# Two thirds of a block's closing gate-and-adds move from VectorE to ScalarE and Pool

## The reference

```python
x = x + g_f * peer_ffn(modulate(rmsnorm(x, norm_ffn_w[i]), sh_f, sc_f), ...)

def block(xc):                                   # 128 tokens at a time
    ...                                          # scores, two top-16s: 8 heads x 16 experts of 16384 for each token
    g = jax.nn.softmax(best_s, axis=-1).astype(xc.dtype)
    act = jax.nn.gelu(jnp.einsum("cd,chkd->chk", xc, u_tab[e]))
    return jnp.einsum("chk,chkd->cd", g * act, v_tab[e])
```

## Time and profile before

| | us |
|---|---|
| median of 3 runs (lowest to highest) | 2940.29 (2937.99 to 2942.69) |
| the profiled execution's own time | 2935.12 |
| its span | 2933.3 |
| TensorE busy | 2632.2 (90%) |
| VectorE busy | 1990.6 (68%) |
| Pool busy | 1349.4 (46%) |
| ScalarE busy | 1043.5 (36%) |

### The profile page before, as it was taken

How to read it: one execution, slowest core, us unless ns; L and a number is a source line. 1 busy time by engine, 2 the same in 40 slices (tenths; PEclk the granted TensorE clock), 3 DMA queues, 4 the chain that set the end, 5 groups by cost and what they waited for, 6 DMA issues and landing times. The chain is left out here.

```text
span 2933.3 us, 36691 instructions
## 1 busy us (share of the span) xinstructions
PE 2632.2 (90%) x12550; PEld 2159.5 (74%) x12550; DVE 1990.6 (68%) x4287; ACT 1043.5 (36%) x2939; POOL 1349.4 (46%) x1076
## 2 busy tenths in 40 slices
PE   4789889999999999999965888999999999999992
PEld 2544558888888888888854766888888887878881
DVE  2356249998877866666674247998877775666667
ACT  3335142269878700000004423229888830000000
POOL 0000034455666666666550005365666674655562
PEclk7889999999999999999987989999999999999996
DMA  7247133799999999999991223599999999999995
GB/s 304 65 189 303 43 116 130 289 384 380 356 410 409 409 404 409 409 409 409 409 375 57 86 71 117 207 374 366 360 384 409 407 407 404 409 409 409 409 409 212
DMA packets 246591, 917.87 MB, mean 313 GB/s; under 512 B 27120, under 2 KB 32272, under 8 KB 239120
## 3 DMA queue, kind: packets, MB, share of 16 engines
q0 software_dynamic: 147456, 536.94, 46.6%
q1 hardware_dynamic: 94800, 374.54, 33.1%
q10 hardware_dynamic: 4160, 4.19, 0.4%
HBM read 909.27 MB, written 6.29 MB: 312 GB/s over the span
## 5 line engine op out<-in xcount | busy, mean ns | idle before, releaser
L1199 PE MATMUL exp_down<-peer_gates,all_ring 128*128 128x256 f32 x2720 | 613.3, 382 | 22.3 <-DMA all_ring<-in_peer_v 22.3
L1172 PE MATMUL exp_out<-peer_both,all_ring 128*128 128x256 f32 x2752 | 617.4, 380 | 9.4 <-DMA all_ring<-in_uT 5.7
L1199 PEld LDWEIGHTS exp_down<-peer_gates,all_ring 128*128 128x128 f32 x2720 | 508.0, 190 | 117.1 <-DMA all_ring<-in_peer_v 50.5
L1172 PEld LDWEIGHTS exp_out<-peer_both,all_ring 128*128 128x128 f32 x2752 | 515.9, 190 | 83.1 <-DMA all_ring<-in_uT 11.8
L1090 POOL DMA_INDIRECT all_xT<-in_u_rows,peer_eidx x278 | 350.4, 1260 | 169.6 <-DVE peer_dots L1548 115.6
L1555 DVE SCALAR_TENSOR_TENSOR peer_both<-all_xT,peer_dots,peer_both 128x1024 f32<-128x1024 f32 x226 | 290.3, 1285 | 147.7 <-DMA all_xT<-in_peer_v,peer_eidx 144.1
L1548 DVE CUSTOM_DVE_ANT_0 all_xT<-all_xT,peer_both 128x1024 f32<-128x1024 f32 x278 | 338.1, 1222 | 66.9 <-DMA all_xT<-in_u_rows,peer_eidx 65.2
L1063 POOL TENSOR_TENSOR ask_w_lo<-all_ring,ask_w_hi 128x1024 fp32r<-128x1024 f32 x22 | 52.5, 2390 | 675.4 <-ACT ask_w_hi L1227 675.4
L1090 POOL DMA_INDIRECT all_xT<-in_peer_v,peer_eidx x230 | 271.3, 1180 | 176.8 <-DVE peer_both L1555 144.3
L1199 PE MATMUL exp_down<-peer_gates,spare_ring 128*128 128x256 f32 x1376 | 315.6, 382 | 13.9 <-DMA spare_ring<-in_peer_v 13.9
L1299 ACT ACTIVATE spare_heavy<-all_iota_b,spare_index 128x128 f32<-128x128 bf16 x1024 | 314.2, 411 | 0.0
(11 more groups left out here) (288 smaller groups left out, 3843.0 us busy)
## 6 DMA issues: line engine op xcount, KB each, us to landing
all_ring<-in_uT SPq DMA_DIRECT2D x172, 512.0 KB, 6.8
all_ring<-in_peer_v SPq DMA_DIRECT2D x170, 512.0 KB, 6.8
mix_raw<-in_ada_tiles SPq DMA_DIRECT2D x48, 1024.0 KB, 9.6
spare_ring<-in_peer_v SPq DMA_DIRECT2D x86, 512.0 KB
spare_ring<-in_uT SPq DMA_DIRECT2D x84, 512.0 KB
all_ring<-in_w_peer_q SPq DMA_DIRECT2D x22, 512.0 KB, 3.7
all_ring<-in_w_gs_in SPq DMA_DIRECT2D x16, 512.0 KB, 3.7
all_ring<-in_w_in SPq DMA_DIRECT2D x12, 512.0 KB, 3.7
```

The source lines that it names most:

```text
L1172: mm = nc.tensor.matmul(outs[:, c % 2, 0:DENSE], raw[c % R][:, k, :], hd[:, k, :], start=(k == 0), stop=(k == KD - 1))
L1199: mm = nc.tensor.matmul(dn[:, m, :], raw[at % R][:, m, :], gates[:, :, c, :], start=(c == 0 and m % 2 == 0), stop=(c == NKEYS - 1), skip_g ...
```

## The change

ScalarE multiplies by the gate: it reads `dn` (eight 128x256) once the last dense product is done, and block 0's transposed sum (eight 128x128), and writes both to SBUF, into columns 0 to 23 of `gates`, which nobody reads any more by then. Pool adds the old stream and writes `xT`: a dense add behind each of the last eight fetches (slots 504 to 511), then eight adds for block 0. The first dense add also waits for the stream to be back and for slots up to 495 to be used. So that `xT` can be written this early, its four row buffers take no slot from 496 on (`TAIL` = 16). VectorE keeps block 1's eight gate-and-adds; it no longer waits for `s_used` and `s_mm` before them, only for the transposes. Nothing else is changed, and the arithmetic is the same but for the rounding between multiply and add.

```diff
--- before.py
+++ after.py
@@ -944,6 +944,7 @@
         PAIRS = NKEYS // 2
         NEAR = 262
         FIRST_DOTS = 46
+        TAIL = 16
         EARLY = [(31, 0, 44), (39, 0, 60), (47, 0, 76), (55, 0, 88), (66, 60, 112), (74, 60, 128)]
 
         HEADS = [(0, 2), (2, 4), (4, PH)]
@@ -985,7 +986,7 @@
         TOPS = 5 * LATER + 1
         own = hs[:, :, :].rearrange("p k n -> p (k n)").rearrange("p (b d) -> p b d", b=FETCHED)
         rows = [xT[:, 2 * j:2 * j + 2, :].rearrange("p k n -> p (k n)") for j in range(4)] + [q.row[:, :]]
-        spans = [(0, SLOTS)] * 4 + [(FIRST_ROWS, SLOTS)]
+        spans = [(0, SLOTS - TAIL)] * 4 + [(FIRST_ROWS, SLOTS)]
         rows += [q.gates[:, 1, c:c + 8, :].rearrange("p c n -> p (c n)") for c, _, _ in EARLY]
         spans += [(since, until) for _, since, until in EARLY]
         rows += [own[:, 0, :], q.picked[:, :]]
@@ -999,6 +1000,8 @@
         freed_late = [5 + i for i, (_, since, _) in enumerate(EARLY) if since > 0]
 
         acc = own
+        gated_dense = q.gates[:, 0, 0:2 * KD, :].rearrange("p (m b) n -> p m (b n)", b=DENSE // P)
+        gated_picked = q.gates[:, 0, 2 * KD:3 * KD, :]
         gates = q.gates
         outs = r.ps("out", [P, 2, 512])
         dn = r.ps("down", [P, KD, DENSE])
@@ -1026,6 +1029,7 @@
             r.sem(x) for x in ("multiplied", "activated", "half_groups_multiplied", "gates_taken", "turned", "sums_turned"))
         s_routed, s_own = r.sem("routed"), r.sem("own_rows")
         s_share = r.sem("shares_known")
+        s_gated = r.sem("gated")
         s_d, s_less, s_exp, s_pack, s_apart, s_hot, s_eidx, s_used, s_gelu, s_wt, s_spread, s_post, s_res = (
             r.sem(x) for x in ("chain", "less", "exp", "packed", "apart", "hot", "experts_known", "row_used",
                                "dots_activated", "row_weights", "gates_spread", "acts_spread", "residual_added"))
@@ -1097,6 +1101,18 @@
                                         f32(hi[:, k, :]).rearrange("p (b n) -> p b n", b=2),
                                         ALU.subtract).then_inc(s_low, 1)
 
+            def dense_add(m):
+                if m == 0:
+                    pool.wait_ge(s_back, 32)
+                    pool.wait_ge(s_used, SLOTS - TAIL)
+                pool.wait_ge(s_gated, m + 1)
+                nc.gpsimd.tensor_tensor(xT[:, m, PICKED:SEQ], gated_dense[:, m, :], q.back[:, m, :],
+                                        ALU.add).then_inc(s_res, 1)
+
+            def picked_add(m):
+                pool.wait_ge(s_gated, KD + m + 1)
+                nc.gpsimd.tensor_tensor(xT[:, m, 0:P], gated_picked[:, m, :], hd[:, m, 0:P], ALU.add).then_inc(s_res, 1)
+
             split_lo(0)
             for k in range(KD):
                 low(k)
@@ -1107,6 +1123,10 @@
                         fetch(n)
             for n in range(FIRST_ROWS, SLOTS):
                 fetch(n)
+                if n >= SLOTS - KD:
+                    dense_add(n - SLOTS + KD)
+            for m in range(KD):
+                picked_add(m)
 
         @block.tensor
         def _(pe):
@@ -1340,6 +1360,13 @@
             act.wait_ge(s_post, len(POST))
             act.dma_start(q.back[:, :, :], x_dram[:, :, PICKED:SEQ]).then_inc(s_back, 16)
             act.dma_start(hd[:, :, :], x_dram[:, :, 0:PICKED]).then_inc(s_back, 16)
+            act.wait_ge(s_mm, 2 * NKEYS)
+            for m in range(KD):
+                act.activation(gated_dense[:, m, :], dn[:, m, :], ACT.Copy, scale=gate[:, m:m + 1]).then_inc(s_gated, 1)
+            act.wait_ge(s_accT, 1)
+            for m in range(KD):
+                act.activation(gated_picked[:, m, :], turned[0][:, m * P:(m + 1) * P], ACT.Copy,
+                               scale=gate[:, m:m + 1]).then_inc(s_gated, 1)
             act.wait_ge(s_back, 32)
 
         @block.vector
@@ -1601,16 +1628,10 @@
                     spread(SPREAD_AT[i])
                 if i in POST_AT:
                     post(POST_AT[i])
-            dve.wait_ge(s_used, SLOTS)
             dve.wait_ge(s_back, 32)
-            dve.wait_ge(s_mm, 2 * NKEYS)
-            for m in range(KD):
-                nc.vector.scalar_tensor_tensor(out=xT[:, m, PICKED:SEQ], in0=dn[:, m, :], scalar=gate[:, m:m + 1],
-                                               in1=q.back[:, m, :], op0=ALU.mult, op1=ALU.add
-                                               ).then_inc(s_res, 1)
-            for b in range(FETCHED):
+            for b in range(1, FETCHED):
                 dve.wait_ge(s_accT, b + 1)
-                sums = (outs if b == 0 else ps_t)[:, :, :].rearrange("p j n -> p (j n)")
+                sums = ps_t[:, :, :].rearrange("p j n -> p (j n)")
                 at = slice(b * P, (b + 1) * P)
                 for m in range(KD):
                     nc.vector.scalar_tensor_tensor(out=xT[:, m, at], in0=sums[:, m * P:(m + 1) * P],
```

## The result

The changed kernel takes 2954.1 us (median of 6 runs, 2951.39 to 2956.7) beside 2937.65 for the kernel before: a ratio of 1.0054, interval [1.0041, 1.0067], or 16 us slower; the forecast had 4 us, and its range ended at 2951.5.

What follows compares the result with a forecast made beforehand. Rows bound each layer's last 28 us, then VectorE alone the end; -3.1 us there and +5.2 from Pool's adds holding rows give +2.1 per layer, +4.2 on 2940.29: 2944.5 us, range 2937.5 to 2951.5.

Steps and rivals of the forecast that it cites:

- The bound: Block's end: for some 28 us per layer only rows count, VectorE using one each 1.39 us, then VectorE alone for 7.40.
- the gain: Behind the last row: sixteen of 24 closing instructions leave VectorE, 7.40 us becomes 4.28, at most 3.1 us per layer.
- ScalarE's part: ScalarE's sixteen activations before the last rows: 5.4 us, hidden in the 28 us, so no cost.
- the length of the adds: Pool's adds at the block's end: 0.72 us for 256 columns, 0.45 us for 128.
- the sign: Whole kernel: slower, by 2.1 us per layer, 4.2 us for two layers.
- A pair: Pool, slots 504 to 511: one fetch with its dense add takes 1.90 us, against 1.39 per fetch before.
- The forecast's sum: Per layer: end 3.1 us shorter, last row 5.2 us later, net +2.1; +4.2 over two layers.
- rival B: Pool's adds wait out whole VectorE rows, half the turns lost: pair 2.6 us, +9.6 in all, 2949.9; chance 0.12.
- costed at nothing: Rows 499 to 511 on five buffers instead of nine: landing in 4.2 to 4.5 us leaves 0.9 to 1.2 us margin.
- Rival E: Five buffers bind because landing takes over 5.6 us: 2 us per layer on top, +8 in all, 2948.5; chance 0.08.
- the adds beside the rows: VectorE's rows from 501 on: dense adds hold them 8 x 0.52 us, four picked adds 4 x 0.26, together 5.2.
- rival A: Each Pool turn costs VectorE the whole add: 7.6 us, net +4.5 per layer, +9.0 in all, 2949.3; chance 0.18.

Runs made afterwards that it cites:

- one_sbuf_input: Changed kernel with VectorE's rows 500 to 511 taking their second input from PSUM; start of row 499 to end of row 511: 22.2 / 21.6 us (layer 0 / 1).
- buffers_only: Kernel before with only the buffer edit: xT's four row buffers take no slot from 496 on; ratio to before 1.0017 [1.0007, 1.0027].
- picked_on_vector: Changed kernel with block 0's eight gate-and-adds back on VectorE, behind the last row; ratio to before 1.0048 [1.0032, 1.0063].
- adds_nine_buffers: Changed kernel with nine row buffers to the end, Pool's adds writing over the old stream; start of row 499 to end of row 511: 24.8 us per layer.
- adds_behind: Changed kernel with all sixteen Pool adds behind the last fetch; ratio to before 1.0037 [1.0023, 1.0052].

## Why the prediction was wrong

**Right.** The bound (rows, in the last 28 us), the gain (3.1 us forecast; 3.1 and 3.5 measured to the next phase), ScalarE's part at nothing, the length of the adds (0.72 and 0.45 us, measured 0.742 and 0.446), the sign, and that Pool and VectorE take turns on two SBUF inputs (one_sbuf_input).

**Wrong: "A pair is gap 0.16 + fetch 1.0 + 0.02 + 0.72 = 1.90 us".** This is the step that failed. The fetch's price was 1.76. I had allowed the adds to collide with rows, and not the fetches, though the earlier trace rows had 1.08 and 0.94 side by side and the timeline had fetches of 1.3 to 1.98, all of them explained by the running row. A pair of 2.70 puts fetch 511 19 us behind fetch 504 and not 13. The forecast's sum, in which VectorE would be the bound (row 511 landed 4 us before its use), turned round: VectorE waited for each of rows 505 to 510. The pace is close to rival B's 2.6, but by another mechanism: there the add was to wait out the row; here it is mostly the fetch (the adds waited too in 2 of the 8 pairs of layer 0, 1.12 to 1.14 us).

**Wrong: the buffers "costed at nothing".** I took the quickest landing in the trace, 4.2 us, where with five buffers the fetches of that stretch took 5.1 to 6.3 (buffers_only). Rival E gave 2 us per layer above 5.6 us; alone it was 3.5, and I had given it 0.08. Rival and forecast were also taken as alternatives, and they came together: the fetches late by their pace and by the lap. A slip in the chances is small beside that: A, B, E and a quarter of the forecast make 0.485, not 0.45.

**Wrong in size: the adds beside the rows.** 5.2 us of holding were forecast in rows 501 to 511; 3.9 and 4.3 came, but 2.8 of them in one row. Eight adds without a fetch between them did not take turns: row 510, ready at 1547.33, ran when the seventh was done, and the eighth waited for it (1426 ns). The forecast had 0.26 us for each of four rows. Here picked_on_vector says that about half of it was hidden. The dense adds held less than forecast: 0.52 us for each of eight rows was the term, and in layer 0 only rows 501, 503 and 506 were held by them, for 0.29 to 0.44 us, in layer 1 four rows for 0.28 to 0.50; where rows and adds alternate without a pause, in adds_nine_buffers, a row takes 1.56, so it is held for 0.28. So the whole add as the price of a turn (rival A, which the prediction's paragraph on the skill calls "the second rival") is out for the dense adds, whose length is 0.74; for the adds in a row it is near: seven at 0.41 us from one to the next are 2.9 us, beside 2.8 held.

The Trainium skill (SBUF — State Buffer, "Who interferes with whom") holds that a `tensor_tensor` with two SBUF inputs doesn't stall Pool's descriptor writing, since it takes only the read interface of the shared pair; it marks the reason as inferred. I did not draw on it, and it would have led to the same fetch of 1.0 us. The traces differ, for both forms: with a `scalar_tensor_tensor` of two SBUF inputs the fetches wait to its end, and with one of them in PSUM they don't; and in the kernel before 20 of 20 fetches wait for a `tensor_tensor` of two SBUF inputs, and 0 of 18 for one with a PSUM input. The measurement decides. The second half was there to be read before the prediction.

## What to carry to other kernels

Look at the spread of an instruction's duration before you use its mean: fetches of 0.94 to 1.98 us were a wait inside the instruction, and a change that shifts the beat of two engines pays the upper end. Work moved to an engine that only issues DMAs is not free if the bound engine waits for those DMAs; count what is queued behind each moved instruction, and count buffers by the landing time seen in that very stretch. The idle engines to take for such an end are those whose work holds none of the bound engine's: here TensorE and ScalarE gave the 3 us that Pool could not.

## What the runs showed of the hardware

- A Pool indirect fetch that starts while VectorE runs a 128x1024 row with two SBUF inputs ends 0.82 us behind that row's end (up to 1.98 us in all); with none running it takes 0.94. With VectorE's second input in PSUM it takes 0.95 inside a row as well. `tensor_tensor` does the same in the kernel before: 0.82 behind it with two SBUF inputs (20 fetches), 0.94 with one in PSUM (18).
- Pool adds back to back (0.41 us from one to the next) held a waiting VectorE instruction for seven adds, 2.8 us; adds of 128x256 in adds_behind took turns with rows (rows of 1.56 to 1.80 us). Why the short ones did not is open.
- With Pool the last to end, the next phase started 4.96 us behind it, with VectorE the last, 1.15 us (layer 0); 3.9 of the 4.96 lie on Pool before the barrier's first step.
